# Combining sums by accumulating DMA, and a reordered block edge, in a two-block transformer kernel on one Trainium2 core

## The reference

```
x = layer_norm(alpha * x + mix, ln_mix_g[layer], ln_mix_b[layer])             # alpha = 4 ** 0.25
x = layer_norm(alpha * x + cross_attend(x, mem, ...), ln_xa_g[layer], ln_xa_b[layer])
x = layer_norm(alpha * x + conv_ffn(x, w_up, conv_w, conv_b, w_down), ln_ffn_g[layer], ln_ffn_b[layer])

def conv_ffn(x, w_up, conv_w, conv_b, w_down):
    up = x @ w_up
    a, g = up[..., :D_FF], up[..., D_FF:]                                      # D_FF = 2816
    g = causal_dwconv(g, conv_w) + conv_b
    return (jax.nn.gelu(g) * a) @ w_down

# second block
h = rms_norm(x, norm_g) * (1.0 + scale) + shift     # scale, shift from w_ada
proj = h @ w_in                                     # RWKV and banded attention follow
```

## Time and profile before

| | |
|---|---|
| median of 3 runs | 1761.2 us |
| the profiled execution | 1760.65 us, span of its trace 1758.8 us |
| busy: PE, DVE, ACT, POOL | 98%, 63%, 39%, 10% of the span |
| instructions | 27808 |
| DMA | 270.44 MB, 154 GB/s mean |
| granted PE clock | full in all 40 slices |

### The profile page before, as it was taken

The page is one execution under the profiler, slowest core; times in us unless marked ns, Lnnn a source line. Parts: engine busy times, 40 slices in busy tenths (PEclk is TensorE's granted clock), DMA queues, the critical chain, the costliest instruction groups (busy, mean ns, idle before and its releaser), DMA issues.

```text
span 1758.8 us, 27808 instructions
## 1 busy us (share of the span) xinstructions
PE 1728.8 (98%) x11461; PEld 1447.6 (82%) x11461; DVE 1110.8 (63%) x1624; ACT 684.7 (39%) x1045; POOL 184.4 (10%) x246
## 2 busy tenths in 40 slices
PE   8999999999999999999999999999998999999998
PEld 7888988988888879888998888888886767777766
DVE  5567266454568795454726755567988585566784
ACT  5332352232235643213235232223554543345452
POOL 4202001200011112000210200001112000011000
PEclk9999999999999999999999999999999999999999
DMA  9882912973345858833492265455683422112412
GB/s 301 259 217 99 252 39 79 279 230 110 126 138 186 260 166 204 247 97 118 114 283 77 83 204 156 143 183 185 201 277 108 153 65 81 34 43 62 169 37 84
DMA packets 175453, 270.44 MB, mean 154 GB/s; under 512 B 10488, under 2 KB 97780, under 8 KB 174560
## 3 DMA queue, kind: packets, MB, share of 16 engines
q1 hardware_dynamic: 147488, 189.90, 34.2%
q0 software_dynamic: 26368, 73.51, 15.7%
q10 hardware_dynamic: 1472, 5.26, 0.8%
HBM read 253.67 MB, written 61.09 MB: 179 GB/s over the span
## 4 chain that ended last, share of the span: by engine, by line
PE 88%; DVE 7%; issue 2%; ACT 1%; DMA 1%; POOL 1%; SPq 0%; ACTq 0%; DVEq 0%
PE ps L365 26%; PE ps L367 26%; PE ps L366 26%; DVE WL L342 2%; PE ps L1007 2%; PE ps L554 1%; PE ps L2575 1%; PE ps L2595 1%; PE ps L2589 1%; DMA RAW<-ffn_w_down 1%; PE ps L1981 0%; DVE SM L1637 0%; PE ps L2609 0%; DVE LATE L2656 0%; PE ps L2712 0%
## 5 line engine op out<-in xcount | busy, mean ns | idle before, releaser
L342 DVE TENSOR_TENSOR WL<-RAW,WH 128x1024 fp32r<-128x1024 f32 x325 | 393.3, 1222 | 387.7 <-ACT WH L332 387.2
L332 ACT ACTIVATE WH<-RAW 128x1024 fp32r<-128x1024 f32 x325 | 341.0, 1058 | 559.8 <-PE ps L367 450.6
L365 PE MATMUL ps<-XH,WH 128*128 128x512 f32 (+1 forms) x1416 | 524.6, 370 | 2.6 <-DVE WL L342 1.5
L367 PE MATMUL ps<-XH,WL 128*128 128x512 f32 (+1 forms) x1416 | 518.1, 366 | 0.0
L366 PE MATMUL ps<-XL,WH 128*128 128x512 f32 (+1 forms) x1416 | 517.9, 366 | 0.0
L365 PEld LDWEIGHTS ps<-XH,WH 128*128 128x128 f32 x1416 | 267.4, 189 | 50.1 <-issue 5.3
L367 PEld LDWEIGHTS ps<-XH,WL 128*128 128x128 f32 x1416 | 267.3, 189 | 43.3
L366 PEld LDWEIGHTS ps<-XL,WH 128*128 128x128 f32 x1416 | 267.5, 189 | 40.7
L365 PE MATMUL ps<-WH,XH 128*128 128x512 f32 x696 | 279.1, 401 | 7.9 <-DVE WL L342 7.0
L367 PE MATMUL ps<-WH,XL 128*128 128x512 f32 x696 | 271.9, 391 | 0.0
L366 PE MATMUL ps<-WL,XH 128*128 128x512 f32 x696 | 271.6, 390 | 0.0
(11 more groups left out here) (404 smaller groups left out, 2063.7 us busy)
## 6 DMA issues: line engine op xcount, KB each, us to landing
RAW<-ffn_w_up SPq DMA_DIRECT2D x176, 256.0 KB, 3.5
weight_sums<-ffn_w_down POOLq DMA_DIRECT2D x12, 1536.0 KB, 18.5
RAW<-w_in SPq DMA_DIRECT2D x33, 512.0 KB, 3.9
RAW<-xa_wkv SPq DMA_DIRECT2D x32, 512.0 KB, 7.5
RAW<-weight_sums SPq DMA_DIRECT2D x32, 512.0 KB, 4.6
weight_sums<-ffn_w_down POOLq DMA_DIRECT2D x12, 1280.0 KB, 31.1
RAW<-c_w_in SPq DMA_DIRECT2D x24, 512.0 KB, 7.2
LATE<-w_ada SPq DMA_DIRECT2D x24, 512.0 KB, 5.2
```

Source lines behind the costliest of these rows:

```text
L332: e.activation(halves_of(i)[0][:, :, 0:w], raw(i)[:, :, 0:w], ACT.Copy).then_inc(*w_hi.up(i))
L342: e.tensor_tensor(wl[:, :, 0:w], raw(i)[:, :, 0:w], wh[:, :, 0:w].bitcast(F), ALU.subtract).then_inc(*w_lo.up(i))
L365: e.matmul(o, lh, rh, start=start, stop=False)
L367: return e.matmul(o, ll, rh, start=False, stop=stop)
```

## The change

1. *Sums.* `scaled` goes: eight instructions of DVE per layer. In the up stage, behind the gelus of blocks 2 to 5, ACT multiplies one row of XR by alpha in place (`residual_act`). POOL then adds the terms that the down product has ready into XR by eight accumulating DMAs per layer (`combined_pool`), each of 128 x 512 float32, from U and Y or a place for U1 (`sum_place`). DVE waits for them where it adds the rest (s = 26, 27, 28 and row 0). `early_pool` stands behind `combined_pool` in POOL's stream.
2. *Rows.* In `down_dve` rows 0 and 1 leave the loop; all four rows stand behind the last low halves (layer 1: also behind that of the first key chunk). In layer 0 PE turns row 0 where it turned row 1, and row 1 behind the end of "e".
3. *Key weight halves.* `half_of` is shifted by one buffer, so that the high half of the first key chunk waits for the second chunk of "e" instead of its third, and ACT makes it before the square sums. The next two are made between the high parts of the second block's input.
4. *Bias copies.* Three of the four are ACT's, DVE makes number 1.
5. *Last row in halves.* The b pass of row 3 and its square sum run in two halves, POOL adds the two sums (`rms_last_pool`), and xn of row 3 is made by ACT (256 columns) and DVE (768).
6. *Transposes.* Rows 0 to 2 are transposed for k = 0 to 3, then for k = 4 to 7, then row 3. k = 7 of row 2 is issued 11 times, k = 7 of row 3 five times (13 before).
7. *Key product.* For its first chunk `gemm_t` starts on the high part of a k tile and waits for the low part only with the last of the three passes.

```diff
-    half_of = [i % NH for i in range(n_in2)] + [i % 3 for i in range(n_out2 - n_in2)] + [0, 1, 2, 0, 1, 3, 4, 2]
+    half_of = [(i + 1) % NH for i in range(n_in2)] + [i % 3 for i in range(n_out2 - n_in2)] + [0, 1, 2, 0, 1, 3, 4, 2]
...
+            if ready and c == 0:
+                for kt in range(2):
+                    e.wait_ge(*ready(x_hi, kt))
+                    for m in range(nm):
+                        ms = slice(128 * m, 128 * m + 128)
+                        if kt == 0:
+                            for w in ps.vacant((stage, m)):
+                                e.wait_ge(*w)
+                        e.matmul(bs[m][:, 0:ntok], wh[:, kt, ms], XH[:, kt, 0:ntok], start=kt == 0, stop=False)
+                        e.matmul(bs[m][:, 0:ntok], wl[:, kt, ms], XH[:, kt, 0:ntok], start=False, stop=False)
+                    e.wait_ge(*ready(x_lo, kt))
+                    for m in range(nm):
+                        r = e.matmul(bs[m][:, 0:ntok], wh[:, kt, 128 * m:128 * m + 128], XL[:, kt, 0:ntok], start=False,
+                                     stop=False)
+                r.then_inc(*gemm.up(("used", i)))
+                continue
...
+            if 2 <= nb < 6:
+                residual_act(e, l, turned, nb - 2)
...
+    def residual_act(e, l, turned, t):
+        for q in range(2):
+            e.wait_ge(*turn.at((turned, t, q)))
+        e.activation(XR[:, t, :], XR[:, t, :], ACT.Copy, scale=ALPHA).then_inc(*ffn_a.up(("residual", l, t)))
...
+    def sum_place(l, u):
+        return late(512 + 512 * u, 512) if l == 0 else late(4096 + 1024 * u, 512)
+
+    def combined_pool(e, l):
+        n = ("ffn", l)
+
+        def added(name, t, j, src):
+            e.wait_ge(*ffn_a.at(("residual", l, t)))
+            e.dma_start(XR[:, t, 512 * j:512 * j + 512], src, accum_op=ALU.add).then_inc(*comb[name].up((l, t)))
+        for u in range(2):
+            e.wait_ge(*dn_a.at(("u", l, u)))
+            added("x11", u, 0, U[u])
+        for u in range(2):
+            e.wait_ge(*ln_v.at((n, "sum", u)))
+            added("x21", 2 + u, 0, sum_place(l, u))
+        for u in range(2):
+            e.wait_ge(*ln_v.at((n, "y", u)))
+            added("x12", u, 1, Y[u])
+        for u in range(2):
+            added("x22", 2 + u, 1, Y[u])
+
...
-                    if name == "e" and (u, q) in ((0, 5), (1, 3)):
-                        behind(u)
+                    if name == "e" and (u, q) == (1, 3):
+                        behind(0)
+        behind(1)
...
-        hi_to(e, n_in2)
+        hi_to(e, n_in2 + 1)
         for t in range(3):
             square_act(e, t)
+            if t == 2:
+                bias_act(e, 0)
             xn_act(e, t)
-        bias_act(e, 0)
-        bias_act(e, 1)
-        square_act(e, 3)
-        hi_to(e, n_in2 + 2)
-        xn_act(e, 3)
-        hi_to(e, n_in2 + 3)
+        bias_act(e, 2)
+        bias_act(e, 3)
+        for half in range(2):
+            square_last_act(e, half)
+        xn_last_act(e)
...
-                if s == 20:
+                if s == 21:
                     e.wait_ge(*dn_a.at(("u", l, u)))
-                    scaled(u, 0, U[u]).then_inc(*ln_v.up((n, "x11", u)))
-                if s == 21:
                     e.wait_ge(*gemm.at(("down", l, 6, u)))
-                    e.wait_ge(*ln_v.at((n, "x11", u)))
-                    e.tensor_tensor(U[u], U[u], ps.tile(("down", l, 6, u))[:, :], ALU.add).then_inc(
+                    if l:
+                        e.wait_ge(*tok_out.at((l, 10)))
+                    e.tensor_tensor(sum_place(l, u), U[u], ps.tile(("down", l, 6, u))[:, :], ALU.add).then_inc(
                         *ps.empties(("down", l, 6, u), ln_v, (n, "sum", u)))
                 if s == 22:
                     e.wait_ge(*ln_v.at((n, "sum", u)))
                     e.wait_ge(*gemm.at(("down", l, 5, u)))
-                    e.tensor_tensor(Y[u], ps.tile(("down", l, 5, u))[:, :], U[u], ALU.subtract).then_inc(
+                    e.tensor_tensor(Y[u], ps.tile(("down", l, 5, u))[:, :], sum_place(l, u), ALU.subtract).then_inc(
                         *ps.empties(("down", l, 5, u), ln_v, (n, "y", u)))
-                if s == 23:
-                    e.wait_ge(*ln_v.at((n, "y", u)))
-                    scaled(u, 1, Y[u]).then_inc(*ln_v.up((n, "x12", u)))
-                if s == 24:
+                if s == 26:
                     e.wait_ge(*gemm.at(("down", l, 7, u)))
-                    scaled(2 + u, 0, ps.tile(("down", l, 7, u))[:, :]).then_inc(*ln_v.up((n, "ax21", u)))
-                if s == 25:
-                    scaled(2 + u, 1, Y[u]).then_inc(*ln_v.up((n, "ax22", u)))
-                if s == 26:
-                    e.wait_ge(*ln_v.at((n, "ax22", u)))
+                    e.wait_ge(*comb["x21"].at((l, 3)))
+                    e.tensor_tensor(x(2 + u, 0), x(2 + u, 0), ps.tile(("down", l, 7, u))[:, :], ALU.add).then_inc(
+                        *ln_v.up((n, "x21", u)))
+                if s == 27:
+                    e.wait_ge(*comb["x22"].at((l, 3)))
                     e.tensor_tensor(x(2 + u, 1), x(2 + u, 1), ps.tile(("down", l, 7, u))[:, :], ALU.subtract).then_inc(
                         *ps.empties(("down", l, 7, u), ln_v, (n, "x22", u)))
-                if s == 27:
-                    e.wait_ge(*ln_v.at((n, "ax21", u)))
-                    e.tensor_tensor(x(2 + u, 0), x(2 + u, 0), U[u], ALU.add).then_inc(*ln_v.up((n, "x21", u)))
                 if s == 28:
                     e.wait_ge(*gemm.at(("down", l, 2, u)))
+                    e.wait_ge(*comb["x11"].at((l, 1)))
                     add(2, u, 0)
                     stats_of(u, 0)
...
-            if s == 30:
-                row(0)
-            if s == 31:
-                row_end(0)
-            if s == 32:
-                row(1)
-            if s == 33:
-                row_end(1)
...
+        lo_to(e, i0 + 35 + NH + l)
         if l:
-            lo_to(e, n_in2)
             e.wait_ge(*ada_v.at(("mod", 5)))
             e.scalar_tensor_tensor(out=s1, in0=mod[:, 8:16], scalar=1.0, in1=VEC[:, vcol["ng"]:vcol["ng"] + 8],
                                    op0=ALU.add, op1=ALU.mult).then_inc(*rms_v.up("s1"))
-            for t in range(2, 4):
+            for t in range(3):
                 row(t)
-                if t == 3:
-                    bias_dve(e, 2)
-                row_end(t)
-            bias_dve(e, 3)
-            e.wait_ge(*rms_g.at(3))
-            lo_to(e, n_in2 + 1)
+                if t:
+                    row_end(t - 1)
+                row_g(t)
+            row_end(2)
+            row(3)
+            last_row_dve(e, n)
+            xn_last_dve(e)
             return
+        row(0)
+        row_g(0)
         lo_to(e, i0 + 36 + NH)
+        row_end(0)
+        row(1)
+        row_g(1)
         turn_dve(e, n, 0)
+        row_end(1)
         row(2)
+        row_g(2)
         turn_dve(e, n, 1)
         lo_to(e, i0 + 37 + NH)
         row_end(2)
         row(3)
+        row_g(3)
         lo_to(e, i0 + 38 + NH)
         row_end(3)
         lo_to(e, i0 + 39 + NH)
+
+    def last_row_dve(e, n):
+        x, g, b = XR[:, 3, :], GB[:, 0:1024], GB[:, 1024:2048]
+        e.wait_ge(*latest["V"])
+        e.bn_aggr(mv[:, 3, :], stats[:, 3, 0:2, :]).then_inc(*ln_v.up((n, 3, "aggr")))
+        bias_dve(e, 1)
+        e.wait_ge(*ln_v.at((n, 3, "aggr")))
+        e.scalar_tensor_tensor(out=x, in0=x, scalar=mv[:, 3, 0:1], in1=g, op0=ALU.subtract,
+                               op1=ALU.mult).then_inc(*ln_v.up((n, 3, "g")))
+        e.wait_ge(*ln_v.at((n, 3, "g")))
+        e.wait_ge(*ln_g.at((n, 3)))
+        for half in range(2):
+            cs = slice(512 * half, 512 * half + 512)
+            e.scalar_tensor_tensor(out=x[:, cs], in0=x[:, cs], scalar=rs[:, 3:4], in1=b[:, cs], op0=ALU.mult,
+                                   op1=ALU.add).then_inc(*ln_v.up((n, 3, "half", half), (n, 3)))
...
+    sqa = SM[:, 252:253]
+
+    def square_last_act(e, half):
+        cs = slice(512 * half, 512 * half + 512)
+        e.wait_ge(*ln_v.at((("ffn", 1), 3, "half", half)))
+        e.wait_ge(*latest["A"] if half else rms_a.at(("sq", 2)))
+        e.activation(SCR[:, cs], XR[:, 3, cs], ACT.Square, accum_out=ss[:, 3:4] if half else sqa).then_inc(
+            *rms_a.up(("sq", 3, half)))
+
+    def xn_last_act(e):
+        e.wait_ge(*rms_g.at(3))
+        e.activation(xn[:, 3, 0:256], XR[:, 3, 0:256], ACT.Copy, scale=rq[:, 3:4]).then_inc(*rms_a.up(("xn", 3)))
+
+    def xn_last_dve(e):
+        e.wait_ge(*rms_g.at(3))
+        e.tensor_scalar(xn[:, 3, 256:1024], XR[:, 3, 256:1024], rq[:, 3:4], None, ALU.mult).then_inc(*rms_v.up(("xn", 3)))
+
+    def rms_last_pool(e):
+        e.wait_ge(*rms_a.at(("sq", 3, 0)))
+        e.tensor_scalar(sqa, sqa, 1.0 / D, 1e-6, ALU.mult, ALU.add).then_inc(*rms_g.up("ms half"))
+        e.wait_ge(*rms_g.at("ms half"))
+        e.wait_ge(*rms_a.at(("sq", 3, 1)))
```

(35 more changed lines are left out.)

32 lines of the change are left out of this document (8 added, 24 removed).

## The result

The changed kernel takes 1765.8 us (median of 14 runs, 1764.74 to 1766.89) where the kernel before takes 1761.84 (14 runs, 1760.03 to 1763.56): a ratio of 1.0023, 95% interval 1.0016 to 1.0030. It is 4.0 us slower, which is clear of the noise. The forecast was 1762.6 (+1.4) with a range of 1758.0 to 1766.5, so the time lies in the range, 3.2 us above the point and close to its upper end.

The account below looks back on a forecast made before the run. PE, busy 98% of the span, was taken to bound the kernel, with 7.1 us of stall to win. Layer 1's +0.4 and layer 0's +1.0 gave +1.4, so 1762.6 us; range 1758.0 to 1766.5.

Parts of the forecast that it names:

- the clock: Layer 1's edge: a 4.5 us PE standstill lowers the clock, giving 1764.7 us; chance 0.2.
- the DMAs: Layer 1's down stage: accumulating transfers delay weight chunks, 4 us of stall, giving 1766.6 us; chance 0.08.
- What bounds the kernel: Last down product "e": PE waits for weight halves queued on busy DVE; 4.3 and 2.8 us, 7.1 in all.
- Layer 0, +1.0 forecast: Half of chunk c0/1 starts at 670.5 behind the rows and PE waits for it; bounds +0.1 and +1.5.
- Layer 1, +0.4 forecast: Down stage and edge: 4.3 us of stall won, 4.7 given back by late rows; bounds -2.2 and +2.2.
- The DMAs, "covered", 0: Residual sums: each transfer lands in 5 us, covered by 3 us or more before DVE wants it; cost 0.
- rival (b): Layer 1, 1315 to 1336: eight transfers beside the loads delay w_down chunks, 4 us of stall, 1766.6; chance 0.08.
- Layer 0's share is lower: Argument against the slower-by-DMA case, set against the 13.9 us of a 1.5 MB accumulating transfer; no size given.
- rival (a): Layer 1's edge: clock falls in the standstill, transposes and key matmuls at half pace, 2.1 us more, 1764.7; chance 0.2.
- The start of the key product, 0: Layer 1's first key chunk: starting on the high half alone, counted in the sum, saves the 0.7 us of XL.
- loops of 4.58, 4.59 and 5.43 us for 4.6, 4.7 and 5.3: Layer 1's rows: b pass to next b pass through ACT and POOL; three loops in the open, before only one.
- (c), the gain: POOL doesn't bind, rows run at DVE's pace: 1759.1, chance 0.16; rows 2 and 3 hidden too: 1754.1, chance 0.08.

Follow-up runs that it names:

- sums_on_dve: The changed kernel with the eight sums back on DVE, no accumulating DMA and no scaled residual: 1766.35 us.
- row1_out_ordered: row1_out with POOL's norm of row t+1 ahead of the RMS of row t in layer 1, and row 0 turned sooner in layer 0: 1760.5 us.
- row1_out: sums_on_dve with row 0 normed between the weight halves again; row 1 stays behind the last half: 1761.69 us.
- early_late: The changed kernel with the four early bias-product loads held back on POOL until the second half of p2 of layer 1 is done: 1764.85 us.
- act_order: row1_out_ordered with ACT's stream reordered (bias copies, row 3's Squares before xn 2), PE's transposes reordered and 23 repeats bridging the gap: 1758.15 us.
- pool_order: The kernel before with POOL's norm of row t+1 ahead of the RMS of row t in layer 1: 1765.0 us.
- row1_out_filled: row1_out_ordered with 12 and 16 more repeats of a transpose in two PE gaps at layer 1's edge: 1759.45 us.
- fill_gap: The changed kernel with 40 more repeats of the third transpose of layer 1's edge: 1768.93 us.

## Why the prediction was right, and where it was not

**The number.** +1.4 was forecast and +4.0 measured. Two rivals, the clock (1764.7) and the DMAs (1766.6), enclose the measured 1765.8, and each came in part. The range held because it reached up to where they stood, not because the forecast's own sum was near: in the traces its +1.4 stands beside +4.9, and all but 0.2 us of the gap is in layer 1.

**What bounds the kernel.** PE without a wait for WL in "e", and nothing gained: as predicted. The cause of the stall was read half right. That DVE is busy 9.93 of the 10 us from 1320 was true and said little: with the eight sums gone the halves are as late. The prediction counted sums and rows together as what frees the halves, and sums_on_dve shows that the rows alone do it. That didn't move the forecast, but the sums were then judged by the DVE time they save.

**Layer 0, +1.0 forecast, +1.16 measured.** The half of c0/1 starts at 670.85, forecast 670.5 and 0.26 of shift brought along; PE waits 1.20 us for it. PE also stands 0.71 and 1.30 us shortly before, which the forecast didn't have; this half comes last and sets the time. By row1_out_ordered the loss hangs on when PE turns row 0: turned sooner, with row 0 in the loop, layer 0 is 2.33 us shorter than in row1_out.

**Layer 1, +0.4 forecast, +3.76 measured.** Three terms were mis-sized:

- *The DMAs, "covered", 0: 1.8.* The forecast took a landing time of 5 us and tested only whether XR is there when DVE wants it. It was, but for 0.9 us in layer 1 and 0.5 in layer 0. What failed is that the transfers share the engines with the weight chunks and, in layer 1, with the early loads, which were costed at 0 too: from 1298 to 1335 the 256 KB loads of w_down land in 7.6 us (median), 3.2 before. This is rival (b) at under half its price, in the place it named. The 1.8 are what both sums_on_dve and early_late win back. "Layer 0's share is lower" held: there the eight are hidden while the rows stand behind the halves.
- *The clock, left to rival (a): about 0.5.* The standstill came as stepped through, 4.44 us for 4.5 forecast, and the clock fell. The rival's 2.1 us were too many: most transposes at half pace lie beside the chain Square, POOL, xn. Its mechanism should have been in the sum, since its own condition ("if the standstill exists at all") was read off the forecast's own order.
- *The start of the key product, 0: 0.74.* From its first matmul to the table load it is 30.47 us in after and in act_order. Before, from the start "as if at 1368.86", it is 29.73. Starting on the high part takes PE through all four banks at once on the first tile, and the third and fourth are still being emptied by the affine passes of DVE and ACT (`vacant`). PE's timeline in after:

```profile
1374.71 0.50 PE L389 MATMUL ps<-XH,WH 128*128 128x512 f32 x1 [0.24 <-DVE SCR L1947]
...
1375.40 0.50 PE L389 MATMUL ps<-XH,WH 128*128 128x512 f32 x1
```

So part 7 loses here about the 0.7 us that the forecast had it save. That is read from code and timeline; no run undoes it alone.

The sum of the traces closes: 1.42 of shift and 2.06 of wait and restart in p3 put the forecast's key product (1369.25) at 1372.73; it starts at 1373.30, 0.57 later, of which 0.5 are the clock. Then 0.39 (forecast) + 2.06 + 0.57 + 0.74 = 3.76. The rest was as stepped through: row 0's add at 1347.94 (1344.4 and 3.48 of shift make 1347.9), loops of 4.58, 4.59 and 5.43 us for 4.6, 4.7 and 5.3.

The port rule quoted from the Trainium skill (SBUF — State Buffer, Who interferes with whom) agrees with the later traces too: POOL's pow takes 0.55 to 0.57 us alone, 1.39 to 1.44 beside a DVE pass over two SBUF tensors, and 1.06 beside the two half passes (row1_out_ordered).

**The rivals.** (c), the gain, needed POOL not to bind. It did bind, and freeing it alone (pool_order) made ACT bind. Of a fall in mid-kernel the trace of before had no row. Now there are some: 0.58 and 0.50 behind the standstill of after, 1.00 in row1_out_filled, where repeats fill the gaps. The rule quoted from the Trainium skill (TensorE: Matmul & The Clock Gate, What's actually happening), that the throttled state is the default and activity releases it, agrees with them.

**Still open.** How the 1.8 us of the DMAs divide between bytes and order on the engines: no run changed the size of the eight. What parts 3 and 7 do alone was read from timelines only. Why the untouched stretch of layer 1 loses 0.2 to 4.3 us in some executions was not tried. fill_gap's time stands against its trace.

## What to carry to other kernels

Take work off a full engine only behind its last wait for the engine that bounds the kernel: ahead of it the time saved becomes waiting (5.5 us saved, 0.03 and 1.13 gained here). A transfer isn't free because its result is in time; ask which loads it delays, and keep other loads out of its stretch. Where several files follow each other (DVE, ACT, POOL, PE), a new order on one of them pays only when the next one's file is put in the same order, and it can pay to fill a gap of PE with idle work (2.15 us in row1_out_filled, 0.5 in fill_gap's stage).
